# Opening of a two-layer trunk kernel: single-slice stages first, weights fetched in halves, padding multiplies on TensorE

## The reference, cut to what matters

```python
# x: 128 context tokens and 256 latent tokens, d_model 2048, 2 layers, all float32
mod = silu(cond) @ w_ada[l] + b_ada[l]          # (2048,) @ (2048, 6144)
shift, scale, gate = split(mod, 3)
h = rmsnorm(x, norm_pre[l]) * (1 + scale) + shift
proj = h @ w_in[l]                              # (384, 2048) @ (2048, 5120)
# ... attention and Fourier mixing (layer 0), pooling and gating (layer 1) ...
x = x + gate * rmsnorm(o @ w_out[l], norm_post[l])
```

## Time and profile before

| | |
|---|---|
| median of 3 runs | 1225.6 us (1225.44 to 1225.65) |
| the profiled execution, its own time | 1227.19 us |
| its span in the trace | 1225.4 us |
| PE busy | 1167.2 us, 95% |
| DVE, ACT, POOL busy | 516.0, 421.9, 16.5 us |
| 16 DMA engines | 234.91 MB, mean 192 GB/s |

### The profile page before, as it was taken

How to read it: one execution, slowest core, us unless ns; L and a number is a source line. 1 busy time by engine, 2 the same in 40 slices (tenths; PEclk the granted TensorE clock), 3 DMA queues, 4 the chain that set the end, 5 groups by cost and what they waited for, 6 DMA issues and landing times.

```text
span 1225.4 us, 14045 instructions
## 1 busy us (share of the span) xinstructions
PE 1167.2 (95%) x5692; PEld 884.0 (72%) x5692; DVE 516.0 (42%) x798; ACT 421.9 (34%) x653; POOL 16.5 (1%) x33
## 2 busy tenths in 40 slices
PE   3899999999999999999999699999999999999994
PEld 0465677777777777777777377788888888878883
DVE  3345465445455442243332553325534433343333
ACT  3323243333355342233322572222333222233331
POOL 0000010000000000010000000000000000000000
PEclk9999999999999999999999799999999999999998
DMA  9999974447355465457755734643344344333413
GB/s 330 337 318 294 296 248 137 181 149 298 138 199 214 180 240 220 158 208 291 271 222 188 313 134 177 243 153 130 129 138 134 107 137 137 117 109 119 137 35 104
DMA packets 106993, 234.91 MB, mean 192 GB/s; under 512 B 4737, under 2 KB 37537, under 8 KB 98097
## 3 DMA queue, kind: packets, MB, share of 16 engines
q1 hardware_dynamic: 104304, 224.41, 51.9%
q0 software_dynamic: 2192, 7.49, 1.9%
q10 hardware_dynamic: 432, 2.11, 0.5%
HBM read 230.32 MB, written 3.67 MB: 191 GB/s over the span
## 4 chain that ended last, share of the span: by engine, by line
PE 92%; DVE 2%; ACT 2%; DMA 2%; issue 1%; SPq 0%; DVEq 0%; ACTq 0%
PE bank L676 26%; PE bank L678 25%; PE bank L677 25%; PE bank L637 4%; PE bank L698 2%; PE bank L784 1%; DVE x L1123 1%; DMA raw_first<-in_w_ada 1%; PE bank L767 1%; DMA raw<-in_w_in 1%; PE bank L734 1%; PE bank L829 1%; PE bank L728 1%; PE bank L774 1%; PE bank L795 1%
## 5 line engine op out<-in xcount | busy, mean ns | idle before, releaser
L676 PE MATMUL bank<-w_hi,h_op 128*128 128x512 f32 x1152 | 475.2, 413 | 4.2 <-DVE h_op L1227 4.2
L678 PE MATMUL bank<-w_hi,h_op 128*128 128x512 f32 x1152 | 452.6, 393 | 0.0
L677 PE MATMUL bank<-w_lo,h_op 128*128 128x512 f32 x1152 | 451.1, 392 | 0.0
L1076 DVE TENSOR_TENSOR w_lo<-raw,w_hi 128x1024 fp32r<-128x1024 f32 x224 | 272.5, 1222 | 268.5 <-ACT w_hi L866 268.0
L866 ACT ACTIVATE w_hi<-raw 128x1024 fp32r<-128x1024 f32 x224 | 234.5, 1054 | 243.6 <-PE bank L678 236.1
L676 PEld LDWEIGHTS bank<-w_hi,h_op 128*128 128x128 f32 x1152 | 217.7, 189 | 92.9 <-issue 51.3
L678 PEld LDWEIGHTS bank<-w_hi,h_op 128*128 128x128 f32 x1152 | 217.3, 189 | 48.9
L677 PEld LDWEIGHTS bank<-w_lo,h_op 128*128 128x128 f32 x1152 | 218.1, 189 | 40.6 <-issue 1.0
L676 PE MATMUL bank<-w_hi,o_low 128*128 128x512 f32 x192 | 76.4, 398 | 0.0
L678 PE MATMUL bank<-w_hi,o_low 128*128 128x512 f32 x192 | 74.9, 390 | 0.0
L677 PE MATMUL bank<-w_lo,o_low 128*128 128x512 f32 x192 | 74.9, 390 | 0.0
(11 more groups left out here) (166 smaller groups left out, 711.7 us busy)
## 6 DMA issues: line engine op xcount, KB each, us to landing
raw<-in_w_in SPq DMA_DIRECT2D x80, 1024.0 KB, 5.2
raw<-in_w_ada SPq DMA_DIRECT2D x64, 1024.0 KB, 7.3
raw_first<-in_w_ada SPq DMA_DIRECT2D x64, 512.0 KB, 5.9
raw<-in_w_out SPq DMA_DIRECT2D x32, 1024.0 KB, 5.1
x<-in_x_sample SPq DMA_DIRECT2D x2, 1024.0 KB, 9.5
out_y_sample<-x SPq DMA_DIRECT2D x8, 256.0 KB, 3.1
x<-in_x_prompt SPq DMA_DIRECT2D x1, 1024.0 KB, 5.0
bias_rows<-in_ada_rows POOLq DMA_DIRECT2D x4, 256.0 KB, 2.9
```

The source lines that it names most:

```text
L676: pe.matmul(out, operand(layer, kind, 0, k, t), hi, start=k % group == 0, stop=False)
L677: pe.matmul(out, operand(layer, kind, 0, k, t), lo, start=False, stop=False)
L678: last = pe.matmul(out, operand(layer, kind, 1, k, t), hi, start=False, stop=k % group == group - 1)
L1076: dve.tensor_tensor(w_lo[:, half % WRING, :, :].rearrange("p k n -> p (k n)"), src, hi, ALU.subtract)\
```

## The change: what it does

- **Stages.** The first two stages hold one K slice each, with two entries of 256 columns (`ks = 8` slices of w_ada rows to an entry, rows of 512 B in the DMA) in place of four; the seven stages behind them are as before. Bytes and entries (32) in all stay the same.
- **Order of steps.** The opening goes in rounds of three halves, one of each chunk, in the order (2, 0, 1), (1, 0, 2), and so on; the first round is taken step by step, (2,0) (0,0) (2,1) (0,1) (1,0) (1,1). Spills follow the new stays of chunks 1 and 2 in their banks: nine in place of eight.
- **Weights.** In the opening a load fetches one half (512 KB) in place of two, into the same four slots. The order of entries and weight loads on SP is written out.
- **Padding.** `warm(n)` issues n full float32 multiplies, 128x128 by 128x512, of the padded condition tile with itself into bank 0, which nothing reads: 14 ahead of the first entry, 4 and 1 behind the first two, 6 ahead of the first step.
- **Small ones.** One throwaway square root on ACT loads its table early; DVE takes the norm's scale and first piece ahead of the entries; evacuations at the opening's end move by a step or two.

```diff
+STAGES = [[0], [1]] + [[2 * r, 2 * r + 1] for r in range(1, ROUNDS)]
+ENTRIES = [2 * len(ks) for ks in STAGES]
+def round_order(r):
+    return (2, 0, 1) if r % 2 == 0 else (1, 0, 2)
+OPENING = [(2, 0), (0, 0), (2, 1), (0, 1), (1, 0), (1, 1)]
+OPENING += [(c, 2 * r + i) for r in range(1, ROUNDS) for c in round_order(r) for i in range(2)]
...
     pre(0, "square")
-    for i in range(4):
-        pre(0, "first_ada", 0, i)
-        if i == 1:
-            pre(0, "norm")
-    pre(0, "first_weights")
+    pre(0, "norm")
+    pre(0, "warm", 0, 14)
+    pre(0, "first_ada", 0, 0)
+    pre(0, "warm", 1, 4)
+    pre(0, "norm_rest")
+    pre(0, "first_ada", 0, 1)
+    pre(0, "warm", 2, 1)
     pre(0, "first_cols", 0)
-    for k in range(2):
-        pre(0, "h", 0, k)
-    for i, n in enumerate((0, 1, 2, 2)):
-        first(n, "first_ada", 1, i)
-    first(3, "first_cols", 1)
-    for k in range(2, 4):
-        first(3, "h", 0, k)
+    pre(0, "first_weights", 0)
+    pre(0, "h", 0, 0)
+    pre(0, "warm", 3, 6)
+    pre(0, "first_weights", 1)
+    first(0, "first_ada", 1, 0)
+    first(1, "first_ada", 1, 1)
+    first(1, "first_cols", 1)
+    first(1, "h", 0, 1)
+    for n, i in ((2, 0), (3, 1), (4, 2), (4, 3)):
+        first(n, "first_ada", 2, i)
+    first(4, "first_cols", 2)
+    for k in STAGES[2]:
+        first(5, "h", 0, k)
+    for b in range(3, len(STAGES)):
+        at_ = 6 * (b - 2)
+        for i, n in enumerate((0, 1, 2, 2)):
+            first(at_ + n, "first_ada", b, i)
+        first(at_ + 3, "first_cols", b)
+        for k in STAGES[b]:
+            first(at_ + 4, "h", 0, k)
...
+    def opening_loads():
+        yield from (("first_ada", 0, 0), ("first_ada", 0, 1), ("mm", 0), ("mm", 1))
+        yield from (("first_ada", 1, 0), ("first_ada", 1, 1), ("mm", 2))
+        yield from (("first_ada", 2, i) for i in range(4))
+        yield from (("mm", 3), ("mm", 4))
+        for b in range(3, len(STAGES)):
+            for i in range(4):
+                yield ("first_ada", b, i)
+                if i < 3:
+                    yield ("mm", 3 * (b - 2) + 2 + i)
+        yield ("mm", 3 * ROUNDS - 1)
...
+            def warm(n):
+
+                pe.wait_ge(cond_ready, 2)
+                for _ in range(n):
+                    pe.matmul(bank[0][:, :], cond[:, 0:4, :].rearrange("p k n -> p (k n)"),
+                              cond[:, :, :].rearrange("p k n -> p (k n)"), start=True, stop=True)
```

More of the change, by code:

```diff
@@ L173, in timetable @@
             for t in range(TOKS):
-                put(FIRST - 1, 12 + t, "evac", c, t)
+                put(FIRST - 1, 14 + t // 2, "evac", c, t)
             continue
         if c == SPILLED[0]:
[L178 to L181, removed]
+            first(-4, "evac", c, 1)
+            first(-3, "turn", c, 0)
+            first(-2, "evac", c, 2)
+            first(-2, "turn", c, 1)
+            put(FIRST, 0, "turn", c, 2)
             continue
@@ L234, in places @@
     yield ("pre", 0)
[L235 to L238, removed]
+    for c, s in OPENING:
+        yield ("at", c, s)
+    for c in range(FIRST, len(CHUNKS)):
+        yield ("pre", c)
+        for s in range(KT):
             yield ("at", c, s)
@@ L250, in hybrid_step @@
     assert len(nth_side) == len(side)
-    loads, fetched = [], 2
+    def opening_loads():
[9 more added lines that the diff above has]
+        yield ("mm", 3 * ROUNDS - 1)
+    loads = list(opening_loads())
+    fetched = 3 * ROUNDS
     for p in places():
@@ L257, in hybrid_step @@
             n = NTH_HALF[p[1], p[2] // 2] + (3 if p[1] < FIRST else 2)
[L258 to L262, removed]
+            if n < len(HALVES) and NTH_UNIT[HALVES[n]] == fetched:
+                loads.append(("mm", fetched))
+                fetched += 1
         for e in table.get(p, ()):
[L264 to L267, removed]
             if e[0] == "ada":
                 loads += [("ada", e[1], e[2] + i) for i in range(e[3])]
-    assert [x[1] for x in loads if x[0] == "mm"] == list(range(len(QUARTERS)))
+    assert [x[1] for x in loads if x[0] == "mm"] == list(range(len(UNITS)))
+    assert [x for x in loads if x[0] == "first_ada"] == [e for e in side if e[0] == "first_ada"]
     nth_first = {x: n for n, x in enumerate(x for x in loads if x[0] == "first_ada")}
@@ L652, in k_step @@
                 if k == 0 and c == FIRST + 1:
-                    wait_spilled(pe, SPILLED[1], 3, TOKS - 1)
+                    wait_spilled(pe, len(STAYS) - 1, TOKS - 1)
                 if k == 0 and c > FIRST + 1:
                     wait_acc(pe, c - 2, TOKS - 1)
[L658 to L663, removed]
+                begin, end = 0, KT - 1
+                if c in SPILLED:
+                    stay = NTH_STAY[c, k]
+                    begin, end = STAYS[stay][1:]
+                    if k == begin and stay:
+                        wait_spilled(pe, stay - 1, TOKS - 1)
                 if k % 2 == 0:
@@ L880, in norm_x @@
                         .then_inc(x_squared, 1)
+                    if layer == 0 and t == 0:
+                        act.wait_ge(x_squared, 1)
+                        act.activation(junk[:, 0:1], stat[:, 4, 0:1], ACT.Sqrt)
                 act.wait_ge(x_mean, layer + 1)
@@ L1379, in part @@
                     norm_x(0)
-                    for j in range(PIECES):
+                    norm_piece(0)
+                elif what == "norm_rest":
+                    for j in range(1, PIECES):
                         norm_piece(j)
```

142 lines of the change are left out of this document (73 added, 69 removed).

## The result

The changed kernel takes 1234.71 us (median of 4 runs, 1233.55 to 1235.22), the kernel before in the same set 1225.62 us (4 runs, 1225.44 to 1225.91). The ratio is 1.007, with a 95% interval of 1.0055 to 1.0085: it is slower, by 9.1 us. The direction was forecast, and the size was not: 1228.5 us was said, 1233 as the upper end.

What follows compares the result with a forecast made beforehand. PE was taken as bound by its multiplies except in its first 60 us. Step 6 at 65.0 plus 123.9 put chunk 3 at 188.9, +2.9 us, so the median goes from 1225.6 to 1228.5 us, range 1224.0 to 1233.0.

Steps and rivals of the forecast that it cites:

- Padding is 0.86 us each, ends at 20.6: Start on PE: 14 paddings of two passes each, 12.0 us plus 2.2 for the lower clock, precede the first entry.
- rival "one pass": A padding multiply takes 0.43 us, so the 25 last 10.8 us less and the kernel is faster, 1222.8 us; chance 0.10.
- Data don't bind the start: First four entries: data land several us early at 3.5 us per MB, so padding, not data, sets the pace.
- The rival of slow rows: Entries of 512 B rows take 7 us each, (1,1) lands at 43.6, all shifts by 6.5, 1235 us; chance 0.08.
- Step 2 at 42.8, at 4.1 us: Stage 2: 3.7 us of transposes and waiting lower the clock, so step 2 takes 4.1 us, to 46.9.
- The chain through load 3: Ahead of (2,3): its load waits for (2,0)'s product; weight load 3, subtraction and (2,1)'s add follow, to 57.8 (55.8).
- the prediction's signs: Trace signs: first step near 32.7, third near 42.8, largest new wait before (2,3), DMA nearly idle 45 to 48.
- chunk 3 near 189: End of the opening: chunk 3 starts at 188.9 against 186.0 before, +2.9 us, with ends +0.6 and +5.0.
- Step 6 "at 67.1, or 62.7 where the level never falls. I take 65.0: one of the two falls, or both briefly": Step 6's start: 67.1 with lower-clock periods at step 2 and around (2,3) and step 5, 62.7 without; 65.0 taken.
- The rest of the opening takes 123.9 again: Step 6 to chunk 3: two more entries, +2.0 us, against 2.2 us of ACT waits gone; 123.9 us unchanged.
- The sum is made against the profiled execution and 1.6 taken off: Profiled execution goes from 1227.19 to 1230.1 us; it stands 1.6 above the median, giving a median of 1228.5.
- The clock holds in both gaps, +0.6: Rival: the clock level never falls at stage 2's gaps, so no difference, +0.6 us, 1226.2; chance 0.24.

Runs made afterwards that it cites:

- e1: The changed kernel with all 25 padding multiplies removed; 1231.02 us, ratio 1.003 to the kernel before.
- e2: The changed kernel with weight load 3 issued ahead of entry (2,3); 1227.66 us, ratio 1.0005 to the kernel before.
- e11: The changed kernel, padding and load order kept, with entries (2,0) to (2,2) multiplied one step earlier; 1224.87 us, ratio 0.9986.
- e4: The changed kernel with three more paddings behind slice 1's transposes, in the gap ahead of step 2; 1232.3 us, ratio 1.0045.
- e9: The changed kernel with padding cut to 8, 2, 1, 1 and weight load 3 ahead of (2,3); 1221.04 us, ratio 0.995.
- e3: The changed kernel without padding and with weight load 3 ahead of entry (2,3); 1222.03 us, ratio 0.9961.
- e7: e9 with three more paddings behind slice 1's transposes, in the gap ahead of step 2; 1219.7 us, ratio 0.9939.
- e10: e9 with entries (2,0) to (2,2) multiplied one step earlier; 1218.93 us, ratio 0.9933.
- e12: e10 with one padding multiply put back behind (2,0) in the gap; 1219.68 us, ratio 0.9944.
- e13: e10 with no padding at all; 1221.29 us, ratio 0.995.

## Why the prediction was right and where it failed

Each step by its forecast and by the rows of after:

- *Padding is 0.86 us each, ends at 20.6; (0,1) from 25.0; step 0 at 32.7.* Measured 20.76, 25.40, 32.66. Right: two passes, and it can't be skipped. The rival "one pass" is out. e1 shows the price at the start, 6.5 us.
- *Data don't bind the start; 512 B rows take 3.5 us per MB.* Right. In e1 the first two entries are 3.42 us apart, bound by data. The rival of slow rows (7 us) is out. Its sum had a slip besides: with (1,1) landing at 43.6 and due at 38.1 the shift is 5.5 us, not 6.5.
- *Step 2 at 42.8, at 4.1 us; (2,0) done at 47.9.* 43.41 (the wait is 2.50) and 48.2. The level fell in the middle of step 2, not ahead of it: of nine multiplies the last three are 0.43 us apart, and (2,0) takes 1.94. The end is right within 0.3 us because errors offset: 0.6 late at the start, step 2 in 3.0 and not 4.1, (2,0) 0.9 longer.
- *The chain through load 3: landed at 54.8, subtraction to 57.1, add to 57.8, (2,3) done at 59.7, step 5 at 60.9, to 64.5.* 55.3, 57.7, 58.3, 60.1, 61.69, to 65.5. Every link was there in the order given, each 0.4 to 1.0 us later. e2 and e11 cut the chain at two places and the wait vanished both times, so this is shown. The wait before (2,3), the idle DMA from 45 to 48 and the places of the first and third step came as the prediction's signs had them; chunk 3 near 189 didn't.
- ***Step 6 "at 67.1, or 62.7 where the level never falls. I take 65.0: one of the two falls, or both briefly".* This step failed.** Both periods came, 1.5 us in step 2 with (2,0) (4.8 against e4's 3.3) and 2.4 in (2,3) with step 5 (1.8 and 3.8 against 1.1 in e4 and 2.2 in e2), and step 6 began at 68.31, 1.2 beyond the upper end. It then ran at the lower level itself until 71.9 (its multiplies 0.43 us apart, where 0.23 is the full pace), a third period that the sum didn't have. The choice of a middle between two worked ends had no row behind it: the gaps had been worked out as 3.7 and 3.8 us (they are 3.8 and 3.5), and the one gap of 3.5 us in the trace had cost the level. That row said 67.1. The forecast would then have been 1230.6, inside the range and still 4.1 us below what was measured; the rest lies in the terms below.
- *The rest of the opening takes 123.9 again.* 123.99 (68.31 to 192.30), and in part by luck. As forecast, two more entries (+2.0) stand against the 2.2 us of waits for ACT, which are gone, and the spills and the smaller halves cost no wait of PE. But the third period at the lower level, in step 6 (3.73 us in place of 2.27), added 1.5 that the sum didn't have; a turn (0.36 us on PE) moved from the opening into chunk 3, where it is part of what the marker adds; and some 0.9 more was saved that no row here takes apart.
- *The sum is made against the profiled execution and 1.6 taken off.* This failed as well, by 1.7 us: the distance of one execution to its median was carried over to another kernel as if it were a constant. After's profiled execution is 0.1 below its median.
- *The clock holds in both gaps, +0.6.* Out: the level fell in or behind both. No run shows this case by itself; in e11, where the level holds (step 6 at 60.00), the chain is cut as well.

So the mechanism was right, and its sizes were not. The misses are 3.3 us in where step 6 starts (2.1 of them the choice of 65.0 over 67.1, 1.2 the links of the chain), 1.2 behind it (0.1 up to chunk 3, 0.6 from there to the marker, 0.5 after it; 7.4 of span in place of 2.9 is 4.5), and 1.7 in the reference: 6.2 in all, 1234.7 less 1228.5.

## What to carry to other kernels

Filler on an in-order engine costs its full length as soon as the data is early, so cut it to the holes of the trace, and look first for real work to put there: an entry moved one step held the level as three paddings did, and freed a slot as well. When an order is rewritten, ask of every load what waits ahead of it in its queue: one entry's slot wait, and the weight load behind it, cost more than 25 padding multiplies. And where a chain gives two ends that hang on a yes or no (the level falls or it doesn't), take the side that the nearest row shows, not the middle.

## What the runs showed of the hardware

- Padding keeps the level through a wait: with three float32 multiplies ahead of step 2, it ran at full clock (e4), and without them it fell in step 2. It isn't regular, though: with the same 3.8 us of transposes and waiting ahead of step 2, the level was down from its first multiply in e1, e2 and e9 (0.43 us apart), and fell at about the seventh of nine in the changed kernel and in e3. Ahead of step 6, 2.0 us of waiting behind 0.8 us of transposes cost the level in the changed kernel, e1, e3 and e7, and didn't in e2, e9, e10, e11, e12 and e13. I had not expected the time of the fall to move so; it is the likeliest reason, not a shown one, why executions of these kernels spread by 2 to 6 us (1226.67 to 1232.49 in e1).
- Rows of 512 B moved 1 MB in 3.42 us, 307 GB/s (e1; 290 GB/s in a window with only such rows, 14 to 18 us), less than the 351 of 1 KB rows and the 383 of 2 KB rows. The Trainium skill ("DMA: Bandwidth & Descriptors", "Specifications") has transfers from 512 B up at line rate; by the runs here rows of 512 B are 20 to 24% short of what 2 KB rows reach.
